# A pair's mixing put ahead of its attention step on TensorE, in a two-model kernel on one core

## The reference, cut to what matters

```python
def _stick_breaking(x, w_q, w_o, k_sb, v_sb):          # k_sb, v_sb = x @ w_kv
        z = jnp.einsum('bhqd,bhkd->bhqk', qblk, k_sb) * scale
        log_one_minus = jnp.where(mask, jax.nn.log_sigmoid(-z), 0.0)
        tail = lax.cumsum(log_one_minus, axis=3, reverse=True) - log_one_minus
        a = jnp.where(mask, jnp.exp(jax.nn.log_sigmoid(z) + tail), 0.0)
        return jnp.einsum('bhqk,bhkd->bhqd', a, v_sb)   # then o @ w_o
...
def _peer(x, w_pq, sub_keys, u, v):                     # 128 experts a token
        u_sel = jnp.take(u, idb, axis=0)
        h = jax.nn.gelu(jnp.einsum('td,ted->te', xblk, u_sel), approximate=False)
        v_sel = jnp.take(v, idb, axis=0)
        return jnp.einsum('te,ted->td', gb * h, v_sel)
```

## Time and profile before

| | |
|---|---|
| median of 3 runs | 2927.89 us (2926.19 to 2929.56) |
| the profiled execution: time, span | 2929.83 us, 2928.0 us |
| PE busy | 2552.8 us, 87% of the span |
| DVE, ACT, POOL busy | 58%, 33%, 22% |
| moved by DMA | 790.63 MB, 270 GB/s on average |
| windows 0 to 3 | about 200 to 1640 us of the span |

### The profile page before, as it was taken

How to read it: one execution, slowest core, us unless ns; L and a number is a source line. 1 busy time by engine, 2 the same in 40 slices (tenths; PEclk the granted TensorE clock), 3 DMA queues, 4 the chain that set the end, 5 groups by cost and what they waited for, 6 DMA issues and landing times.

```text
span 2928.0 us, 30820 instructions
## 1 busy us (share of the span) xinstructions
PE 2552.8 (87%) x10701; PEld 1629.5 (56%) x10701; DVE 1700.9 (58%) x3833; ACT 953.0 (33%) x1946; POOL 637.1 (22%) x625
## 2 busy tenths in 40 slices
PE   8887777799887899877777888999899899998999
PEld 4563222264452565522222356995699568975798
DVE  3547776756667556667665456544555555536554
ACT  1423222234222253322222234432444344423443
POOL 0014444423344323334444010001000000002000
PEclk9999999999999999999999999999999989999999
DMA  7139999999999989999999432543154404523352
GB/s 291 58 135 421 422 421 422 420 415 375 421 421 421 404 341 381 420 416 421 421 420 418 188 115 101 188 171 144 58 189 156 172 31 173 186 112 115 130 186 101
DMA packets 113203, 790.63 MB, mean 270 GB/s; under 512 B 16995, under 2 KB 19766, under 8 KB 22070
## 3 DMA queue, kind: packets, MB, share of 16 engines
q0 software_dynamic: 73760, 536.93, 44.6%
q1 hardware_dynamic: 39318, 252.16, 22.9%
HBM read 787.97 MB, written 1.07 MB: 269 GB/s over the span
## 4 chain that ended last, share of the span: by engine, by line
PE 64%; DMA 22%; DVE 7%; ACT 3%; issue 3%; POOL 1%; DVEq 0%; SPq 0%; ACTq 0%; POOLq 0%
DMA weights<-in_peer_uv,scratch 14%; PE psum L965 13%; PE psum L1236 13%; PE psum L1189 13%; PE psum L1250 12%; DMA arena<-in_peer_uv,scratch 8%; PE psum L1038 3%; PE psum L1046 2%; DVE heads_arena L2046 2%; PE psum L952 2%; PE psum L1024 1%; PE psum L975 1%; PE psum L1002 1%; PE psum L1013 1%; ACT scratch L1544 1%
## 5 line engine op out<-in xcount | busy, mean ns | idle before, releaser
L1189 PE MATMUL psum<-weights,scratch 128*128 128x512 f32 x1224 | 591.3, 622 | 161.1 <-ACT scratch L1544 161.1
L1189 PEld LDWEIGHTS psum<-weights,scratch 128*128 128x128 f32 x1224 | 229.4, 196 | 489.4 <-ACT scratch L1544 248.1
L1189 PE MATMUL psum<-arena,scratch 128*128 128x512 f32 x824 | 398.6, 618 | 108.8 <-ACT scratch L1544 108.8
L2479 POOL DMA_INDIRECT weights<-in_peer_uv,scratch x306 | 338.9, 1108 | 510.8 <-PE psum L1189 485.3
L2298 DVE TENSOR_TENSOR piece<-weights,piece 128x2048 fp32r<-128x2048 f32 x128 | 292.8, 2293 | 221.1 <-ACT piece L1626 221.1
L965 PE MATMUL psum<-weights,xT 128*128 128x512 f32 (+2 forms) x936 | 400.5, 585 | 13.3 <-ACT xT L1413 6.9
L1236 PE MATMUL psum<-split_x,piece 128*128 128x256 f32 x3072 | 386.2, 287 | 6.2 <-DVE split_x L2305 6.2
L1236 PEld LDWEIGHTS psum<-split_x,piece 128*128 128x128 f32 x3072 | 384.2, 196 | 11.6 <-issue 7.6
L1250 PE MATMUL psum<-piece,hidden 128*128 128x512 f32 x1536 | 358.8, 390 | 0.0
L1536 ACT ACTIVATE scratch<-scratch 128x2 f32<-128x2 f32 x256 | 52.0, 203 | 886.2 <-DVE heads_arena L2046 882.4
L1189 PEld LDWEIGHTS psum<-arena,scratch 128*128 128x128 f32 x824 | 154.2, 195 | 330.3 <-ACT scratch L1544 171.0
(11 more groups left out here) (220 smaller groups left out, 2460.8 us busy)
## 6 DMA issues: line engine op xcount, KB each, us to landing
weights<-in_w_up SPq DMA_DIRECT2D x64, 1024.0 KB, 4.8
weights<-in_w_down SPq DMA_DIRECT2D x64, 1024.0 KB, 4.8
weights<-in_w_kv_b SPq DMA_DIRECT2D x16, 1024.0 KB
weights<-in_w_qkv_a SPq DMA_DIRECT2D x6, 2048.0 KB, 16.2
weights<-in_a_w_in SPq DMA_DIRECT2D x6, 2048.0 KB, 10.1
weights<-in_w_q_b SPq DMA_DIRECT2D x8, 1024.0 KB
weights<-in_w_o_b SPq DMA_DIRECT2D x8, 1024.0 KB
weights<-in_peer_w_q SPq DMA_DIRECT2D x8, 1024.0 KB
```

Of the source, the lines that this page charges most:

```text
L1189: mm = pe.matmul(psum[g.bank][:, :], diagonal[:, n % DIAGONALS, :], row[:, D + half * BANK:D + (half + 1) * BANK], start=(k == 0), stop=(k ...
L2479: pool.indirect_dma_start(gathered[n % GATHER_SLOTS], None, rows, bass.IndirectOffsetOnAxis(ap=expert[:, w % NT, k:k + 1], axis=0), elemen ...
```

## The change

On PE, M(p) is put ahead of S(p) in windows 1 and 2; before, S(p) came first. Some of the later steps of the attention are put one pair further on: `stick_softs` from f+2 to f+3, `stick_less_later` and `stick_exps` from f+4 to f+5, `stick_values` from f+5 to f+6, and `STICK_OUT` and all after it by one. The steps `stick_piece` (one pair behind PE), `stick_logs` (f+1) and `stick_later` (f+3) stay at their pairs.

```diff
-STICK_OUT = 32
-STICK_NORM_STEPS, STICK_NORM_ROOT = (37, 39, 40, 41), 38
-QUERY_TURN, QUERY_PIECES, QUERY_SCORES = 42, 44, 49
-ROUTE_NEXT, GATE_NEXT, SHARES_NEXT = (52, 53, 54, 55, 57, 59, 60, 62), (55, 61), (57, 63)
+STICK_OUT = 33
+STICK_NORM_STEPS, STICK_NORM_ROOT = (38, 40, 41, 42), 39
+QUERY_TURN, QUERY_PIECES, QUERY_SCORES = 43, 45, 50
+ROUTE_NEXT, GATE_NEXT, SHARES_NEXT = (53, 54, 55, 56, 57, 59, 60, 62), (56, 61), (58, 63)
...
@@ PE, stick_step
-                    if pair == first + 5:
+                    if pair == first + 6:
                         copied(s.v[(2 * j + 1 if t == 0 else j)].group)
                         for b in both:
                             stick_values(s, b)
@@ PE, experts
                         if w == 0:
                             second_queries(peer0, pair)
-                        elif w <= NT:
+                        mix(w, pair)
+                        if 0 < w <= NT:
                             stick_step(stick[w - 1], pair)
-                        mix(w, pair)
@@ ACT, stick_step
-                    if pair == first + 4:
+                    if pair == first + 5:
                         stick_exps(s, both)
-                    if pair == first + 6 and 2 * (j + 1) % (s.n // 2) == 0:
+                    if pair == first + 7 and 2 * (j + 1) % (s.n // 2) == 0:
                         stick_outputs(s, 2 * j // (s.n // 2))
@@ DVE, stick_step
-                    if pair == first + 2:
+                    if pair == first + 3:
                         stick_softs(s, both)
-                    if pair == first + 4:
+                    if pair == first + 5:
                         stick_less_later(s, both)
```

## The result

The changed kernel takes 3084.02 us (median of 5 runs, 3079.59 to 3086.22) where the kernel before took 2929.56 us beside it: a ratio of 1.0532, 95% interval 1.0520 to 1.0544. It is 154 us slower; 3045 was predicted, with 2960 to 3090 as the range.

The account below looks back on a forecast made before the run. Transfers were taken to set the pace, with PE the chain's bound at 7.0 us a pair. Window 1 34, window 2 60, projections 41, cushion -18 gave 117 us: 3047 on the profiled execution, median 3045, range 2960 to 3090.

Parts of the forecast that it names:

- hidden: Rival for windows 1 and 2: cushion and slots absorb all stalls under the transfers, time stays at 2928 us; chance 0.05.
- faster: Rival for windows 1 and 2: slots come free up to 3.5 us earlier, say 20 us back, 2908 us; chance 0.05.
- milder: Rival: copies, gates and projections hide in the transfers' time; only logs, their clock and early start show, 2959 us; chance 0.10.
- Larger: Rival: clock also stays low for the piece behind a stall, or the queries run dry, 3085 to 3120 us; chance 0.08.
- Piece: PE idle behind each piece until ACT's copy and diagonals: 0.85 us, query piece 1.2; 13 us in each window.
- Logs: PE idle behind each batch's scores, waiting for ACT's stick_logs: 7.4 us, less earlier idle; 31 us for logs over both windows.
- Adds: Output projection, DVE's adds ahead of the next weigh: stalls of 3.4, 5.0, 6.1, 3.4 us; 15.4 us more each window.
- DVE's softs: Window 2, second half of softs waits for PE's values: 7.1 us idle at pairs 20 and 28, 4.4 at 24; 18.6 us.
- Clock: Mixes behind new stalls over 3.5 us run 1.7 us longer: 5 us window 1, 7 window 2, 10 projections.
- Queries: Four query pieces, 1.1 us each, and the scores behind them stay under the cushion: 0, or 3 us each window.
- Cushion: About 8 us of queued transfers absorb PE's lateness: 3 us off each attention part, 6 off each projection, 18 us in all.
- Early start: M(10) no longer stands behind S(10): 3.5 us gained once in each of windows 1 and 2.

Follow-up runs that it names:

- the order alone: Kernel before with M(p) put ahead of S(p), every ACT and DVE step left at its old pair: 3117.36 us, ratio 1.0655.
- the kernel with the followers moved: Changed kernel with ACT's copies and logs and DVE's adds one pair further on, PE's values one pair earlier: 2927.85 us, ratio 0.9999.
- the adds and copies: Two runs on the changed kernel: only DVE's four projection adds one pair later, 3042.79 us; only ACT's copies, query pieces included, one pair later, 3033.89 us.
- the kernel with the clock kept: Changed kernel with 3, 5, 6 and 3 idle matrix products on PE ahead of mixes 34 to 37 of windows 1 and 2: 3078.20 us, ratio 1.0505.
- The moves alone: Changed kernel with its later pairs kept, but PE's step again ahead of the mix of its pair: 2932.46 us, ratio 1.0017.
- The four edits: On the changed kernel, one at a time: copies later 3033.89 us, logs later 3075.12 us, adds later 3042.79 us, values earlier 3060.11 us.
- the pair of copies and logs: Changed kernel with ACT's copies and logs both one pair further on: 3000.38 us, ratio 1.0247.

## Why the prediction was right, and where its sizes were off

**The cause.** The step on which all rests, that the diagonals of M(p+1) stand in ACT's list behind the copy of S(p) and the cover of 7 us becomes zero, is shown: by the idle times with their releaser, by the order alone (+6.5%) and by the kernel with the followers moved (no loss). The rivals are out: hidden and faster by the result, milder by the adds and copies, which cost 45 and 47 us. Larger is out as it was told: the pieces of both windows (lines 1038 and 1046) took 147.6 us before and 147.5 after, so none ran slow behind a stall. But its other half, that the query pieces cost, came true in part. The forecast stood 39 us under the measured 3084, which is only 6 us inside the range: the mechanism was right, and the terms below were too small.

**The stalls one by one.** Most were right in the second digit. Piece: 0.85 and 1.2 predicted, 0.85 and 1.38 seen. Logs: 7.4 and 7.4; with the gate 9.0 and 9.03; pair 18 7.0 and 7.28. Adds: 3.4, 5.0, 6.1, 3.4 and 3.45, 5.04, 6.10, 3.46. DVE's softs at pair 20 of window 2: 7.1 and 6.45. A query piece was short, since the diagonals start 0.90 us behind the start of its first copy (611.07 to 611.97), not 0.75. The softs were long by 0.65 us at pairs 20 and 28 and by 0.6 at pair 24, which has no routing step: DVE starts them 0.35 us before PE ends its values, and `weigh` starts 2.29 us behind the start of the two products, not 2.46.

**Table loads.** The sum had 1.28 us for a load, and the chain after has it so, with the next instruction 0.01 us behind. The larger price of the Trainium skill, ScalarE: Activation LUTs, section What ACT_TABLE_LOAD costs (about 2.66 us with a drain), would have made the logs' stall 11.5 us (7.4 + 3 x 1.38, an estimate from that page); it was 7.4.

**Clock, mis-sized.** The step "1.7 us for the new stalls over 3.5 us: 5 + 7 + 10 us" gave 22 us. The mixes ran 49 us longer. The reason is in the rows: the prediction took 5.40 us for a slow mix from one stall of 4.06 us; here mixes behind 3.5 to 9 us of idle took 5.1 to 6.8. In the 8 us from 799 to 807, with the mix of 6.76 us, the granted clock was 0.57 of the full 2.4 GHz, so most of that mix ran at 1.2 GHz. The eight mixes of the projections alone took 51.8 us where they took 30.6 before, 21 us for the 10 of the sum. Which part of the 49 us the time bears was tested at these eight only: they ran 22 us shorter in the kernel with the clock kept, and the time fell by 8 us, with 6 of uncertainty.

**Queries, missed.** The prediction let the four query pieces stay under the cushion, 0 or 3 us. The mixes fell back by 14.7 and 17.2 us, of which 5.7 and 8.0 are the new order's own and no loss, and some 9 the stalls. Besides the four copies a gate stands behind the copy at pair 46, a stall of 3.90 us, which the sum did not have. Of the 9 us 3.9 and 5.0 were left when the next window began; moving the copies gave back 7 us in all.

**Cushion, too large.** Against the kernel with all followers moved, 3.9 and 2.4 us are taken back behind the projections, where 6 were predicted, and it hides none of the stalls: each is idle time of PE in full.

**Early start, nothing.** The sum had -3.5 us in each window for M(10) ahead of S(10). The kernel with all followers moved has this start too and is as fast as the kernel before (0.9999, 0.9990 to 1.0009): it only moves the mixes' places, and gives back no time that can be measured.

**By place**, by the last column of the table of both kernels. Up to pair 33 the prediction had 34.5 and 60.5 us, without the early start and after 3 us of cushion; seen were 42.2 and 62.4 (130.0 - 67.6). The projections, net of what is taken back by pair 45: 14.4 each predicted, 21.5 and 23.0 seen. The queries and what follows: 0, and 3.9 and 5.0. So 124 against 158; the prediction's 117 are these 124 less 7 for the early start.

**One sign was wrong.** "Line 2085 waits far less than now" did not come: DVE waits 41.9 us there for PE's later steps, after 43.4. The moves alone brought it down to 13.2 us, and the order alone put it up to 76.0, so the room that the moves give is used up by the order.

**Parts do not add up.** The four edits alone give 47, 11, 45 and 25 us, 128 of the 156 us that they give together. Nearly all of the missing 28 us is shown by the pair of copies and logs: 84 for both, 57 added.

## What to carry to other kernels

In a software pipeline written out by hand, swapping two blocks on one engine moves every wait of the others by one step; list for each follower what stands between its release and the next block, and move all or none. Here the swap alone cost 6.5%, the swap with half of the followers moved 5.3%, with all of them nothing. A short copy in an in-order engine's list (0.4 us) is cheap only as long as what comes behind it is not needed next: look at what is queued behind the wait, not at the wait. And when a reordering moves where blocks stand, read the loss at a place against a kernel of the same order that has no loss: against the kernel before, 5 to 8 us of each falling back here were none.

## What the runs showed of the hardware

PE's clock made a second cost out of each long stall. Behind 3.45 us of idle a mix took 6.76 us in place of 3.6, while the piece right behind it was already at its usual 3.6 us; with idle products that left gaps of under 1 us (0.75 to 0.95) the same mixes took 3.70 us. So this stall of 3.45 us held PE up for 6.6. The slow mix's extra time was nearly twice that of the prediction's one example (3.1 us against 1.7).
